# The first half's stages behind the projection run in two spans of 256 tokens, the second beside expert turns

## The reference

```
n1 = RMSNorm(x)*(1+scale1)+shift1 ;  h = n1 @ w_in            # 8704 columns
branch A: gated linear recurrence (HGRN2), 4 heads, state 128x128, carried over the tokens
branch B: windowed attention, 3 groups x 4 heads: (window, dilation) = (128,1), (512,4), (2048,16)
x += gate1 * ((sigmoid(gA)*(oA@w_branch_a) + sigmoid(gB)*(oB@w_branch_b)) @ w_out)
n2 = RMSNorm(x)*(1+scale2)+shift2
x += gate2 * PEER(n2)
```

## Time and profile before

| | us |
|---|---|
| median of 3 runs | 4416.77 (4406.45 to 4421.81) |
| span of the profiled execution | 4435.7 |
| TensorE busy | 3251.9 (73%) |
| VectorE (DVE) busy | 2593.4 (58%) |
| ScalarE (ACT) busy | 1955.8 (44%) |
| GpSimd (POOL) busy | 1472.8 (33%) |
| DMA moved | 1447.75 MB, mean 326 GB/s |

### The profile page before, as it was taken

One profiled execution on the slowest core, in us unless ns is written; L12 is line 12 of the kernel. 1 busy time (PEld: TensorE's weight loads), 2 busy tenths in 40 slices (PEclk: granted clock), 3 DMA queues, 4 the chain that ended last, 5 costly groups with the idle time before them and its releaser, 6 DMA issues. The chain is left out here.

```text
span 4435.7 us, 46775 instructions
## 1 busy us (share of the span) xinstructions
PE 3251.9 (73%) x14243; PEld 1706.6 (38%) x14243; DVE 2593.4 (58%) x6557; ACT 1955.8 (44%) x6710; POOL 1472.8 (33%) x1175
## 2 busy tenths in 40 slices
PE   6998868874999999786754687985555555555556
PEld 4677754642543346444432454651111111111111
DVE  2362334476557745584646536656766766766774
ACT  2122431145457734483532225544545545545554
POOL 4543102352322233231212112223444444444443
PEclk8998889986999999787976898987867677777769
DMA  6533244389999999796999978889999999999998
GB/s 258 198 138 129 71 154 171 115 347 356 393 384 356 378 365 387 288 358 232 402 315 383 369 277 308 348 321 383 421 404 421 420 404 415 413 403 414 415 407 334
DMA packets 313374, 1447.75 MB, mean 326 GB/s; under 512 B 42913, under 2 KB 104257, under 8 KB 164770
## 3 DMA queue, kind: packets, MB, share of 16 engines
q0 software_dynamic: 152064, 1107.36, 62.4%
q1 hardware_dynamic: 146690, 330.19, 21.0%
q10 hardware_dynamic: 14368, 7.21, 0.6%
HBM read 1377.25 MB, written 74.57 MB: 327 GB/s over the span
## 5 line engine op out<-in xcount | busy, mean ns | idle before, releaser
L2928 POOL DMA_INDIRECT uv_ring<-in_peer_uv,pick_idx x1024 | 1134.5, 1108 | 2255.1 <-PE expert_acc L3089 1929.2
L3089 PE MATMUL expert_acc<-uv_ring,diag 128*64 128x512 f32 x3968 | 1263.8, 773 | 665.6 <-ACT diag L3059 629.4
L3016 DVE SCALAR_TENSOR_TENSOR uv_ring<-uv_ring,n_pairs 128x1024 f32<-128x1024 f32 x1024 | 1246.5, 1230 | 672.9 <-DMA uv_ring<-in_peer_uv,pick_idx 639.9
L3089 PEld LDWEIGHTS expert_acc<-uv_ring,diag 128*64 128x64 f32 x3968 | 293.8, 163 | 1519.5 <-ACT diag L3059 994.2
L3046 ACT ACTIVATE gelu_cube<-dots_now 128x2 f32<-128x2 f32 x528 | 105.6, 200 | 929.7 <-DVE uv_ring L3016 854.3
L3054 ACT ACTIVATE pick_weight<-gelu_tanh,pick_share 128x1 f32<-128x1 f32 x1056 | 350.8, 379 | 17.6
L3059 ACT ACTIVATE diag<-half_pattern,pick_weight 128x64 f32<-128x64 f32 x1024 | 300.4, 340 | 16.6
L956 PE MATMUL h_acc_q<-in_w_all_q,n_all_q 128*128 128x512 f32 x640 | 286.8, 601 | 0.0
L3049 ACT ACTIVATE gelu_tanh<-gelu_cube,dots_now 128x1 f32<-128x1 f32 x1056 | 253.3, 286 | 16.2
L3051 ACT ACTIVATE pick_share<-dots_now,pick_prob 128x1 f32<-128x1 f32 x1056 | 245.4, 280 | 0.0
L953 PE MATMUL h_acc_q<-n_all_q,in_w_all_q 128*128 128x272 f32 x896 | 218.0, 399 | 10.0 <-DMA in_w_all_q<-in_w_in 10.0
(11 more groups left out here) (457 smaller groups left out, 4784.8 us busy)
## 6 DMA issues: line engine op xcount, KB each, us to landing
in_w_p<-in_w_in SPq DMA_DIRECT2D x34, 1024.0 KB, 7.2
in_w_all_q<-in_w_in SPq DMA_DIRECT2D x17, 2048.0 KB
ada_w<-in_w_ada SPq DMA_DIRECT2D x10, 2048.0 KB, 8.8
uv_ring<-in_peer_uv,pick_idx POOLq DMA_INDIRECT x1024
past_keys_q<-in_past_keys SPq DMA_DIRECT2D x16, 1024.0 KB
past_rows_q<-in_past_values SPq DMA_DIRECT2D x16, 1024.0 KB
score_pair<-scores SPq DMA_DIRECT2D x66, 128.0 KB
wq_raw_p<-in_peer_wq SPq DMA_DIRECT2D x16, 512.0 KB, 5.7
```

Source lines behind the costliest of these rows:

```text
L2928: pool.indirect_dma_start(self.rows_of(part, s), None, self.x["peer_uv"][0], bass.IndirectOffsetOnAxis(ap=self.idx[:, q % 2, s, k:k + 1], ...
L3016: ins = dve.scalar_tensor_tensor(out=row, in0=row, scalar=1.0, in1=self.n2[:, tile % 2, s if tile < LAST_TILE else 0, :], op0=ALU.mult, op ...
L3089: ins = pe.matmul(self.acc[s * 64:(s + 1) * 64, c, :], self.diag[:, part % DIAGS, s, :], rows, start=first, stop=last)
```

## The change

`front` is called three times. The first call does opening norm and projection for tokens 0-511 as before, then hgrn to query for tokens 0-255 (`FIRST_SPAN`, `_a`, split products, no experts but for 14 opening turns in its query stage). The second (`NEXT_SPAN`, `_b`, tokens 256-511) has no norm1 and no projection; its stages are those of the unsplit kind (plain float32, `out_phase`, norm, query with `beside`), and 66 parts (14 to 80) are paced beside them at 66/489. The third (`LAST_SPAN`, `_q`) is the second half as before, from part 80 to 257 at 177/2281, with the query stage's pace at 1.6 instead of 1.18. The gate units of tokens 0-511 all go in the gaps of `_a`, two for each gap that had one. Attention has 6 jobs for 256 tokens: two for each group; a job of dilation 4 has two residues of 64 tokens and one of dilation 16 eight of 16, so its tensors are loaded by two and by eight DMAs. The sixth ring slot serves parts 87 to 151.

```diff
+FIRST_HALF = Span("_p", 0, 512, ((0, 512),), 512, False, True)
+FIRST_SPAN = Span("_a", 0, 256, ((0, 256),), 512, False, True)
+NEXT_SPAN = Span("_b", 256, 256, ((0, 256),), 512, False, False)
+LAST_SPAN = Span("_q", 512, 544, ((0, 272), (272, 272)), 512, True, False)
...
 class Opening(Alone):
-    TURNS = 24
+    TURNS = 14
+    PER_HEAD = 2 + len(FIRST_SPAN.tiles)
     PICKS_FROM, PICKED = 2, 3
-    PICKS = (((0, 0), (0, 1)), ((0, 2),), ((0, 3), (0, 4)), ((1, 0), (1, 1)), ((1, 2),), ((1, 3), (1, 4)))
-    PICK_POINT = 2 + 6 * (PICKS_FROM + 1)
+    PICKS = (((0, 0), (0, 1)), ((0, 2), (0, 3), (0, 4)), ((1, 0), (1, 1)), ((1, 2), (1, 3), (1, 4)))
+    PICK_POINT = 2 + PER_HEAD * (PICKS_FROM + 1)
...
-MORE_FROM, MORE_TO = 33, 125
+MORE_FROM, MORE_TO = 87, 151
...
+LAST_PACE = {query_phase: 1.6}
 MOD_US = 250.0
+NEXT_PARTS = 80
+NEXT_US = 489.0
 FRONT_PARTS = 257
-FRONT_US = 2140.87
+FRONT_US = 2281.0
...
 def hgrn_phase(...):                          # the same on sp, pool, act and pe
+    PER = 4 // N_P
-            beside.gap("pe", 1)
+            beside.gap("pe", PER)
...
 def attention_tiles(span):
+    def stream(r, k, m, n):
+        per = P // k
+        return lambda t: [(slice(e * k, (e + 1) * k), t[0:SEQ, :].rearrange("(i r) c -> r i c", r=r)[m * per + e][n * k:(n + 1) * k])
+                          for e in range(per)]
+    T = span.prompt
+    b = span.first // T
...
+    for g in range(1, G):
+        r = GROUPS[g][1]
+        k = T // r
+        own, before = (M_OWN, M_BEFORE) if k == P else (masks.index((k, True)), masks.index((k, False)))
+        for m in range(r * k // P):
+            out.append((g, stream(r, k, m, b), [(stream(r, k, m, b), own)] + ([(stream(r, k, m, b - 1), before)] if b else []), P // k))
...
 def attention_phase(...):
+    PER = 4 // len(span.full)
-            beside.half_unit()
+            for _ in range(PER):
+                beside.half_unit()
...
 def merge_phase(...):
-            beside.gap("pool", 1)
+            beside.gap("pool", 4 // N)
 def branch_phase(...):
-        if span.samples:
-            weights.first()
+        weights.first()
...
 def front(whole, span, beside, opening, first_gains, coming_span):
+    tag, busy = span.tag, not span.split
+    if span.split:        # opening, projection of `whole` (512 tokens) beside the modulation, as before
+        ...
+        between = InGaps(GateBlocks(nc, here, banks, whole, split_weights, n_hi, n_lo, x, dram))
+    elif whole is not None:                   # norm1 and projection beside experts, as before
+        ...
...
-        first_gains = front(SPANS[0], Alone(), False, opening, None)
+        front(FIRST_HALF, FIRST_SPAN, Alone(), opening, None, None)
         later[0].hold_rows(keep)
-        beside = Beside(later[0], FRONT_PARTS, FRONT_US, Opening.TURNS)
-        front(SPANS[1], beside, True, None, first_gains)
+        beside = Beside(later[0], NEXT_PARTS, NEXT_US, Opening.TURNS)
+        first_gains = front(None, NEXT_SPAN, beside, None, None, LAST_SPAN)
+        beside = Beside(later[0], FRONT_PARTS, FRONT_US, NEXT_PARTS)
+        front(LAST_SPAN, LAST_SPAN, beside, None, first_gains, None)
```

More of the change, by code:

```diff
@@ L455, in first @@
     def first(self):
-        self.load(0)
-        self.load(1)
+        if not self.begun:
+            self.begun = True
+            self.load(0)
+            self.load(1)
 class OutWeights:
@@ L1428, in attention_tiles, with span_masks @@
         m = at // P
[L1429 to L1433, removed]
-    return out
+        out.append((0, window(m), [(window(m), M_OWN)] + ([(window(m - 1), M_BEFORE)] if m else []), 1))
+    masks = span_masks(T)
+    for g in range(1, G):
[4 more added lines that the diff above has]
+            out.append((g, stream(r, k, m, b), [(stream(r, k, m, b), own)] + ([(stream(r, k, m, b - 1), before)] if b else []), P // k))
+    return out
+def span_masks(tokens):
+    return [(P, True), (P, False)] + [(tokens // r, own) for _, r in GROUPS[1:] if tokens // r < P for own in (True, False)]
 def attention_phase(nc, ph, span, beside, const, consts, dram, past_keys, q_s, s_rows):
@@ L1441, in attention_phase @@
     N = len(jobs)
-    E = max(len(keys) for _, _, keys in jobs)
+    PER = 4 // len(span.full)
+    E = max(len(keys) for _, _, keys, _ in jobs)
     NQ = G * WIDTH
@@ L1483, in load_keys @@
                 return
-            g, queries, keys = jobs[j]
+            g, queries, keys, _ = jobs[j]
             s = j % 2
@@ L1522, in _ @@
         for j in range(N):
-            g, queries, _ = jobs[j]
+            g, queries, _, _ = jobs[j]
             load_keys(j + 2)
@@ L1728, in attention_constants @@
     t = np.arange(P)
[L1729 to L1735, removed]
+    for tokens in (BLOCK // 2, BLOCK):
+        kinds = span_masks(tokens)
+        open_ = np.zeros((len(kinds), P, P), bool)
+        for n, (k, own) in enumerate(kinds):
+            if k == P:
+                open_[n] = t[None] <= t[:, None] if own else t[None] >= t[:, None]
+            else:
+                open_[n] = (t[None] // k == t[:, None] // k) & ((t[None] <= t[:, None]) | (not own))
+        out[f"att_masks{tokens}"] = np.where(open_, 0.0, MASKED).astype(np.float32).transpose(1, 0, 2).reshape(P, -1)
     inv = (THETA ** (-np.arange(0, ROT, 2, dtype=np.float32) / np.float32(ROT))).astype(np.float32)
@@ L3200, in build, with front @@
         consts_phase(nc, lambda name: nc.alloc_semaphore(name=name), const)
-        def front(span, beside, busy, opening, first_gains):
+        def front(whole, span, beside, opening, first_gains, coming_span):
             T, N = span.count, len(span.tiles)
-            tag = span.tag
+            tag, busy = span.tag, not span.split
             def held(ctx, name, shape, dt=F32, side="left"):
@@ new lines, in front @@
+                                assert all(n == Modulation.TURNS for n in second.taken.values()), second.taken
+                            here = lambda name, shape: gated.enter_context(nc.sbuf_tensor(name, shape, F32))
+                            banks = lambda name, shape: gated.enter_context(nc.psum_tensor(name, shape, F32))
+                            between = InGaps(GateBlocks(nc, here, banks, whole, split_weights, n_hi, n_lo, x, dram))
+                        elif whole is not None:
+                            n_hi, n_lo = both(gated, "n1")
+                            with ExitStack() as rows:
```

74 lines of the change are left out of this document (30 added, 44 removed).

## The result

| | median us | runs |
|---|---|---|
| before | 4411.61 | 4404.77 to 4421.81, 4 runs |
| changed | 4689.41 | 4679.12 to 4697.76, 4 runs |

The ratio is 1.0613, 95% interval 1.0578 to 1.0648: 278 us slower. The forecast was 117 us slower, with a range that ended at 4625 us. The sign was right, and the forecast size was less than half of the measured one.

The account below looks back on a forecast made before the run. TensorE was taken to bound the second half's projection, DMA nearly full in attention and merge, neither full elsewhere. 396 + 431 + 510 + 1792 + 1424 = 4553 against 4435.7, +117, so 4534 us by median; range 4405 to 4625.

Parts of the forecast that it names:

- Span b: Tokens 256-511 beside 66 parts: 510 us, chosen between two bounds because its pacing is denser than the second half's.
- both bounds: For span b's 181 MB: 470 us at the opening's 385 GB/s, 570 at the second half's rates stage by stage.
- b's own work: Span b's stages without parts, estimated from halved first-half stages, less gate units, and from unsplit products: 332 us.
- Rival 3: In span b, chains bound it, not bytes; late landings delay DVE: b 614, total 4730, chance 0.09.
- Span a, 431: Tokens 0-255, from 396 us until its query ends: 431 us in place of 640.
- the 14 opening parts: In span a's query stage after the first fetch: 5.8 us each, 82 us.
- Span q, -184: Third span with 177 parts for 233: projection saves 54 us, other stages 130, so 1976 becomes 1792.
- The other 28 parts: Parts removed from span q outside the projection: 4.6 us each, 5.25 times a DMA share of about 0.87, saving 130.
- Rivals 1 and 2: 1: DMA queues alone limit everywhere, about 4385 us, chance 0.11. 2: b at its floor, q at its best, 4428, 0.13.
- Rest: The phase after span q: the same 271 parts alone, 1424 us again.
- the masks and picks: Constants loaded once a stage, and picks in four points instead of six on DVE: counted at nothing.
- The rate limit: About 358 GB/s of HBM a core would give span b at least 506 us; left to measurement, the sum unchanged.

Follow-up runs that it names:

- e3: Changed kernel with 33 expert parts in span b instead of 66, the third span taking 47 to 257: 4635.35 us, ratio 1.0488.
- e1: Changed kernel with no expert part in span b, the third span taking parts 14 to 257: 4632.67 us, ratio 1.0466.
- e2: Kernel before, unsplit, with 177 parts in its second half instead of 233 and 56 more in the rest: 4556.41 us, ratio 1.0299.
- e4: Changed kernel; in span b's query stage, weight loads after the first two bring one eighth of their bytes: 4680.97 us.
- e10: Changed kernel; parts 14 to 79 make two of four TensorE products (a tile's first and last part keep all): 4684.3 us.
- e12: Changed kernel with the edits of e8 and e10 at once, half the gathered bytes and half of TensorE's products: 4609.86 us.
- e8: Changed kernel; parts 17 to 79 bring plain 512 KB loads in place of 1 MB gathers: 4610.04 us, ratio 1.0428.
- e14: e13 plus, for parts 14 to 79, two of four TensorE products and six of ten ACT instructions: 4509.22 us, ratio 1.0201.
- e13: Changed kernel; parts 17 to 79 bring 32 KB for each 1 MB gather, dots over 64 columns: 4543.55 us, ratio 1.0278.

## Why the prediction was wrong, point by point

- **Span b, the failed step: "The pacing is denser than in the second half ..., so I lie between: 510."** It measured 602, above both bounds (470 and 570). The upper bound, by bytes over the second half's rate in the same stage, was close stage by stage: hgrn 109 for 99 measured, attention 138 for 142, branch 53 for 51, out 57 for 62, norm 25 for 23, but merge 20 for 31 and query 168 for 194. What failed is the step between the bounds: nothing drew b towards the opening's 385 GB/s. The choice between the bounds cost 60 us; the other 32 are 186 MB instead of 181 and 309 GB/s instead of 181/570 = 318. Denser pacing did raise b's rate, from 243 GB/s with 33 parts (e3) to 309 with 66, but not above the 328 that the prediction has for the second half outside the projection, and the price of a part rose with it, from 3.4 to 4.0 us. The runs show in place of 510: 357 us of b's own and 3.7 a part, of which about two thirds (156 of 245) go when the gathers' bytes go.
- **b's own work:** 332 estimated, 357 measured (e1). As a sum, own work plus price would have been the better form: 357 + 66 * 3.7.
- **Rival 3** named the mechanism (b's in-order chains, point of decision b over 570), and its b of 614 was near the 602. Its total of 4730 was too high, since it let `_q` save only 107 where 157 came. Its words put it on late parts that delay DVE; the runs show that the stages' loads were late, not the parts. The measured 4689 lies in its range (over 4610), to which I had given 0.09.
- **Span a, 431:** measured 454. hgrn (90 for 95), attention (95.5 for 94), merge (17.5 for 18.5) and the 65 us to the first fetch (66.0) held. Missed: branch 46.7 for 40, and the 14 opening parts, 99.5 us instead of 82, or 7.1 each for 5.8. In branch it loads all its weights for half the columns, now at 202 GB/s, but TensorE waits for them only 2.0 us in all; the cause stays open. Beside the opening parts TensorE waits 19.1 us for POOL, which splits the query's weights (4.5 us beside the 24 parts before); that could be most of the 17.5, and so could a start that is paid once. Neither was tried.
- **Span q, -184:** measured -157. The projection fell by 66 us instead of 54, 2.3 us a part. Of that, h_acc_q itself gave 11 (531.42 in rows 4, 520.28 now). The share there fell from 0.96 to 0.84 and TensorE stayed at 0.98, so TensorE bounds it, as said. The other 28 parts gave back 91 us instead of 130: 3.2 each for 4.6. That mistake is of the same kind: the price was a share of the bytes' time. e2 shows the same without a split: there the projection is 60 us shorter with 23 parts fewer, 2.6 each, and the other 33 give back 3.3 to 3.5 each.
- **Rivals 1 and 2** needed b under 440 and near 465. Both fall. **Rest** held to 1 us, and the masks and picks left no mark that I found in these rows.
- **The rate limit.** The Trainium skill's 358 GB/s ("DMA: Bandwidth & Descriptors", Specifications), set beside the sum, isn't the limit here: the rest moved 405 GB/s for 1425 us. The Trainium skill says so itself elsewhere ("Perfetto Trace Analysis", Roofline): when only one core of a pair is active it can pull more than that share, bounded by about 435 GB/s of its 16 DMA engines. By that figure the rest stands at 93%, an estimate.

## What to carry to other kernels

Price background work that is put beside an in-order stage as the stage's own time plus a price per unit, and take that price from a stretch of the same kind, not from the densest one; here it was 3.7 us where the unit alone takes 5.25, and only 2.8 came back where it left (3.1 in e2). Read the time from issue to landing of the stage's small loads, which the gathers turned from 1.9 us into 17.9 here, and the time that their issuing takes. And price the split itself: e1 shows +4.7% with none of the 66 parts in span b. It holds a second pass over the weights, short stages, smaller pieces, unsplit products for 256 tokens and ten opening parts fewer, which no run told apart.

## What the runs showed of the hardware that I had not expected

- In one stage, under gathers of 1 MB, the time to land hardly depended on a load's size: 9.8 us for 64 KB (e4) and 10.4 for 512 KB, which took 4.1 without gathers (e1). It differed more from stage to stage: 17.9 for 32 KB in attention, 4.1 and 5.9 for 256 KB in branch.
- SP issued loads of 32 KB at one in 0.46 us (16 in 7.36 us, e1), and TensorE waited 8.2 us there for loads whose median time to land was 1.8.
- Where TensorE work was left out, the granted clock (a mean over levels of 1.2 and 2.4 GHz) fell too: from 0.80 to 0.72 (e10), 0.84 to 0.75 (e12 against e8) and 0.91 to 0.83 (e14 against e13). In e10 248 of 528 records of the parts went, 68 us at their mean before, and TensorE's busy time fell by 27.
- With the gathers' bytes gone, span b's granted clock was 0.91, above the 0.80 beside them, TensorE being busy for 0.77 of the span instead of 0.63.
